# Differential attention of the second layer: scores from two zero-padded copies of the queries, chunk mask added on VectorE

## The reference, cut to what matters

```python
def diff_attention(xn, cos, sin, in_w, q_norm_g, k_norm_g, ..., subln_g, out_w, lambda_init):
    proj = xn @ in_w
    q = proj[..., :1024].reshape(b, s, 8, 2, 64)
    k = proj[..., 1024:2048].reshape(b, s, 8, 2, 64)
    v = proj[..., 2048:].reshape(b, s, 8, 128)
    q = apply_partial_rope(rmsnorm(q, q_norm_g), cos, sin)
    k = apply_partial_rope(rmsnorm(k, k_norm_g), cos, sin)
    scale = 1.0 / math.sqrt(64)
    for blk in range(2):                       # blocks of 128 queries
        qb = q[:, 128 * blk:128 * (blk + 1)]; kc = k[:, :128 * (blk + 1)]
        sc = einsum("bqhcd,bkhd->bhcqk", qb, kc) * scale
        allowed = k_chunk[None, :] <= q_chunk[:, None]      # chunks of 64 tokens
        p = softmax(where(allowed, sc, -inf), axis=-1)
        attn = p[:, :, 0] - lam * p[:, :, 1]
        out_blk = einsum("bhqk,bkhe->bqhe", attn, vc)
    o = rmsnorm(o, subln_g) * (1.0 - lambda_init)
    return o @ out_w
```

## Time and profile before

| | |
|---|---|
| time, median of 3 runs | 1951.2 us (1949.14 to 1953.17) |
| profiled execution | 1950.13 us |
| its span | 1948.4 us |
| PE busy | 1867.1 us (96%) |
| PE weight loads | 1721.3 us (88%) |
| DVE busy | 1351.8 us (69%) |
| ACT busy | 1008.9 us (52%) |
| POOL busy | 5.2 us |
| HBM read | 306.99 MB, 158 GB/s over the span |

### The profile page before, as it was taken

How to read it: one execution, slowest core, us unless ns; L and a number is a source line. 1 busy time by engine, 2 the same in 40 slices (tenths; PEclk the granted TensorE clock), 3 DMA queues, 4 the chain that set the end, 5 groups by cost and what they waited for, 6 DMA issues and landing times.

```text
span 1948.4 us, 32782 instructions
## 1 busy us (share of the span) xinstructions
PE 1867.1 (96%) x12931; PEld 1721.3 (88%) x12931; DVE 1351.8 (69%) x1733; ACT 1008.9 (52%) x1213; POOL 5.2 (0%) x32
## 2 busy tenths in 40 slices
PE   6988999999999899999999999999999999899998
PEld 6988889998878789989999998999989999799997
DVE  6967678888755588877667667666756666657665
ACT  5734455566534465556445435444545445645443
POOL 1000000000000000000000000000000000000000
PEclk8999999999989999999999999999999999999999
DMA  5632145555423245545555554555646554226552
GB/s 186 192 111 107 65 152 187 176 204 174 153 84 108 87 154 191 191 159 189 185 181 173 173 177 149 197 183 180 195 141 205 177 186 157 86 87 203 183 176 85
DMA packets 237638, 309.15 MB, mean 159 GB/s; under 512 B 8186, under 2 KB 213752, under 8 KB 237560
## 3 DMA queue, kind: packets, MB, share of 16 engines
q1 hardware_dynamic: 236520, 308.03, 47.6%
q10 hardware_dynamic: 1040, 0.03, 0.0%
HBM read 306.99 MB, written 1.05 MB: 158 GB/s over the span
## 4 chain that ended last, share of the span: by engine, by line
PE 85%; DVE 8%; ACT 3%; issue 3%; DMA 0%; SPq 0%; DVEq 0%; ACTq 0%
PE ps L599 22%; PE ps L601 11%; PE ps L626 9%; PE ps L628 9%; PE ps L629 9%; PE ps L578 6%; PE ps L580 6%; PE ps L579 6%; DVE weights_lo L1692 2%; ACT weights_hi L1110 1%; PE ps L859 1%; PE ps L806 1%; PE ps L695 1%; DVE scratch L1742 1%; DVE scratch L1738 1%
## 5 line engine op out<-in xcount | busy, mean ns | idle before, releaser
L1692 DVE TENSOR_TENSOR weights_lo<-raw_weights,weights_hi 128x2048 fp32r<-128x2048 f32 x290 | 663.8, 2289 | 252.6 <-ACT weights_hi L1110 252.0
L599 PE MATMUL ps<-normed,weights_hi 128*128 128x512 f32 x2112 | 749.3, 399 | 2.5 <-DVE normed L1775 2.4
L1110 ACT ACTIVATE weights_hi<-raw_weights 128x2048 fp32r<-128x2048 f32 x290 | 551.7, 1905 | 212.1 <-PE ps L580 88.6
L601 PE MATMUL ps<-normed,weights_lo 128*128 128x256 f32 x2112 | 593.3, 281 | 0.0
L599 PEld LDWEIGHTS ps<-normed,weights_hi 128*128 128x128 f32 x2112 | 397.1, 188 | 97.7 <-DVE weights_lo L1692 2.7
L626 PE MATMUL ps<-down_in_hi,weights_hi 128*128 128x256 f32 x1440 | 413.2, 287 | 19.7 <-DVE down_in_lo L1795 7.0
L628 PE MATMUL ps<-down_in_lo,weights_hi 128*128 128x256 f32 x1440 | 412.0, 286 | 0.0
L629 PE MATMUL ps<-down_in_hi,weights_lo 128*128 128x256 f32 x1440 | 411.7, 286 | 0.0
L601 PEld LDWEIGHTS ps<-normed,weights_lo 128*128 128x128 f32 x2112 | 399.7, 189 | 0.1
L578 PE MATMUL ps<-normed,weights_hi 128*128 128x256 f32 x1088 | 322.3, 296 | 10.0 <-DVE normed L1775 7.1
L579 PE MATMUL ps<-normed,weights_hi 128*128 128x256 f32 x1088 | 311.3, 286 | 0.0
(11 more groups left out here) (244 smaller groups left out, 1362.8 us busy)
## 6 DMA issues: line engine op xcount, KB each, us to landing
raw_weights<-in_ffn_w_gate_up_dram SPq DMA_DIRECT2D x88, 1024.0 KB, 5.1
raw_weights<-in_ffn_up_w_dram SPq DMA_DIRECT2D x44, 1024.0 KB, 5.1
raw_weights<-in_ffn_w_down_dram SPq DMA_DIRECT2D x44, 1024.0 KB, 4.9
raw_weights<-in_ffn_down_w_dram SPq DMA_DIRECT2D x22, 1024.0 KB, 4.9
raw_weights<-in_ssd_in_w_dram SPq DMA_DIRECT2D x20, 1024.0 KB, 5.3
raw_weights<-in_a_w_in_dram SPq DMA_DIRECT2D x14, 1024.0 KB, 5.0
raw_weights<-in_attn_in_w_dram SPq DMA_DIRECT2D x12, 1024.0 KB, 5.1
raw_weights<-in_ssd_out_w_dram SPq DMA_DIRECT2D x8, 1024.0 KB, 4.9
```

The lines of the kernel that those rows point to most:

```text
L599: mm(ps[:, b + a, :], wh[:, k, a * P:(a + 1) * P], h[:, k, :, :].rearrange("p c t -> p (c t)"), start=(k == 0), stop=False, skip_group_che ...
L601: last = mm(ps[:, b + a, 0:T], wl[:, k, a * P:(a + 1) * P], h_hi[:, k, :], start=False, stop=(k == DK - 1), skip_group_check=True)
L1110: f(w_hi[:, s, :], raw[:, s, :], ACT.Copy).then_inc(hi_split.sem, hi_split.plus())
L1692: tt(w_lo[:, s, :], raw[:, s, :], f32(w_hi[:, s, :]), ALU.subtract).then_inc(lo_split.sem, lo_split.plus())
```

## The change

The queries exist twice after it, each copy zero in one half of the partitions, so that a product over all 128 partitions gives the score of one of the two queries. ACT makes the copies in `part_queries`, two activations of 128x512 for each pair of heads, during units 5 to 8 of the projection; `halves` holds the two columns of ones and zeros that scale them. PE's four products a step become two over 128 partitions, and the wait on `first_scored` goes. The mask, now a table of 128x256, is added by DVE with the scale of the scores in one operation from PSUM to `s_buf`; the row maxima and the exponentials read `s_buf`. The scale had been part of the query gain. Three more things move: the values of heads 4 to 7 are turned into banks 0 and 1, after the copies of the first ones and without a wait for the rotation; the memory's inverse root is made after unit 11, into `rstd`, ahead of the value copies on ACT; and PE waits for all copies of values, queries and rotated pairs before its first scores. POOL makes two small fills more at the start.

```diff
+            fill(chunk_mask[0:64, P + 64:T], MASKED)
+            fill(halves[0:64, 0:1], 1.0)
+            fill(halves[64:P, 1:2], 1.0)
...
                     if kind == "diff":
-                        mm(ps[:, b, 0:nk], q[0:64, :], proj[0:64, 8 + h, 0:nk], start=True, stop=False,
-                           skip_group_check=True)
-                        late_keys(b, 0, nk, 0).then_inc(first_scored.sem, first_scored.plus())
-                        return
+                        second = second_q[h // 2][:, h % 2, a * P:(a + 1) * P]
+                        mm(ps[:, b, 0:nk], q, proj[:, 8 + h, 0:nk], start=True, stop=True)
+                        last = mm(ps[:, b, T:T + nk], second, proj[:, 8 + h, 0:nk], start=True, stop=True)
...
-            def scores_second(n):
-                if kind == "diff":
-                    h, a, b = n // 2, n % 2, n % 3
-                    nk = keys_of(kind, a)
-                    pe.wait_ge(first_scored.sem, first_scored.value())
-                    mm(ps[:, b, T:T + nk], proj[64:P, q0 + h, a * P:(a + 1) * P], proj[64:P, 8 + h, 0:nk],
-                       start=True, stop=False, skip_group_check=True)
-                    late_keys(b, T, nk, 64).then_inc(scored.sem, scored.plus())
...
             up_unit(first=True)
-            pe.wait_ge(qk_rotated.sem, qk_rotated.next(2))
-            turn_value(1, 2)
+            pe.wait_ge(evacuated.sem, evacuated.value(-1))
+            pe.wait_ge(values_copied.sem, values_copied.next(2))
+            turn_value(1, 0)
...
+            pe.wait_ge(q_parted.sem, q_parted.next(4))
+            pe.wait_ge(qk_rotated.sem, qk_rotated.next(2))
             pe.wait_ge(values_copied.sem, values_copied.next(2))
-            softmax_attention("diff", diff_step, lambda: pe.wait_ge(values_copied.sem, values_copied.next(2)))
+            softmax_attention("diff", diff_step)
...
-                            last = f(p_buf[n % 2][:, j, 0:nk], ps[:, n % 3, j * T:j * T + nk], ACT.Exp,
+                            last = f(p_buf[n % 2][:, j, 0:nk], s_buf[n % 2][:, j, 0:nk], ACT.Exp,
...
+            def part_queries(j):
+
+                act.wait_ge(qk_rotated.sem, qk_rotated.next())
+                q = proj[:, 2 * j:2 * j + 2, :]
+                f(second_q[j], q, ACT.Copy, scale=halves[:, 1:2]).then_inc(step.sem, step.plus())
+                act.wait_ge(step.sem, step.value())
+                f(q, q, ACT.Copy, scale=halves[:, 0:1]).then_inc(q_parted.sem, q_parted.plus())
...
+                if 5 <= n < 9:
+                    part_queries(n - 5)
...
-                if n == 10:
-                    act.wait_ge(stat_done.sem, stat_done.next())
-                    inverse_root(mem_rstd, ps[:, STAT, 0:T], 1.0 / D).then_inc(rstd_ready.sem, rstd_ready.plus())
...
             skip(11, 0)
+            act.wait_ge(stat_done.sem, stat_done.next())
+            inverse_root(rstd[:], ps[:, STAT, 0:T], 1.0 / D).then_inc(rstd_ready.sem, rstd_ready.plus())
             copy_values(TURNED_BEFORE_DIFF, False)
...
                         dve.wait_ge(scored.sem, scored.next())
-                        v.tensor_reduce(t[:, 1, :], bank(n % 3)[:, :, 0:nk], AX_X, ALU.max,
+                        stt(s[:, :, 0:nk], bank(n % 3)[:, :, 0:nk], scale, rows(chunk_mask[:, T - nk:T], 2),
+                            ALU.mult, ALU.add).then_inc(step.sem, step.plus())
+                        dve.wait_ge(step.sem, step.value())
+                        v.tensor_reduce(t[:, 1, :], s[:, :, 0:nk], AX_X, ALU.max,
                                         negate=True).then_inc(shifted.sem, shifted.plus())
```

More of the change, by code:

```diff
@@ L156 @@
 UNITS = sum(s[4] for s in STREAM)
-POOL_MADE = 9 + 2 + ROPE_HALF + 3 + 2 + 4
+POOL_MADE = 10 + 2 + ROPE_HALF + 3 + 3 + 4
 EARLY_EXTRAS, EXTRAS = 4, 9
@@ L219, in build_program @@
         cols = sb("columns", [P, 64])
+        halves = sb("halves", [P, 2])
         eps_col, lam_col, subln_col, freq_col = (cols[:, i:i + 1] for i in range(4))
@@ L276, in build_program @@
         qk_rn = [scr(3840 + 512 * i, 2, T) for i in range(3)]
-        mem_rstd = scr(5376, T)
+        second_q = [scr(5632 + 512 * i, 2, T) for i in range(3)] + [proj[:, 38:40, :]]
         qk_a, qk_b = proj[:, 34:36, :], proj[:, 36:38, :]
-        query_gain = cols[:, 12:13]
         o_rs = [proj[:, 2 * i:2 * i + 2, :] for i in range(4)]
@@ L471, in _ @@
             for m, v in ((ident, 0.0), (ones, 1.0), (upper, 1.0), (half_ones, 0.0), (swap, 0.0),
-                         (chunk_mask, 0.0), (causal_mask, 0.0), (cols, EPS)):
+                         (chunk_mask, 0.0), (causal_mask, 0.0), (halves, 0.0), (cols, EPS)):
                 fill(m[:], v)
@@ L513, in _ @@
             decay_in = c("decay_in")
-            first_scored = c("first_scored")
             evacuated = c("evacuated")
@@ L534, in _ @@
             qk_rotated = c("qk_rotated")
+            q_parted = c("q_parted")
             qk_squares = c("qk_squares")
@@ L799, in ssd_core, with softmax_attention @@
                 square_sum(3, 6, 0)
-            def softmax_attention(kind, between=lambda n: None, ready=lambda: None):
+            def softmax_attention(kind, between=lambda n: None):
                 n_heads, q0, _, _ = attention(kind)
-                def late_keys(b, at, nk, row):
-                    return mm(ps[:, b, at + nk - 64:at + nk], chunk_mask[row:row + 1, 0:P],
-                              chunk_mask[row:row + 1, P:P + 64], start=False, stop=True, skip_group_check=True)
                 def scores(n):
@@ L866, in softmax_attention @@
                     scores(n)
-                    scores_second(n)
-                ready()
                 for n in range(n_units):
@@ L871, in softmax_attention @@
                         scores(n + 2)
-                        scores_second(n + 2)
                     between(n)
@@ L1075, in _ @@
             qk_rstd = c("qk_rstd")
+            qk_rotated = c("qk_rotated")
+            q_parted = c("q_parted")
             qk_squares = c("qk_squares")
@@ L1357, in copy_values @@
                     a, b = (i // 2, i % 2) if by_token else (i % 2, i // 2)
-                    f(v_tok[:, a, 512 * b:512 * b + 512], ps[:, i, :],
+                    f(v_tok[:, a, 512 * b:512 * b + 512], ps[:, i if by_token else a, :],
                       ACT.Copy).then_inc(values_copied.sem, values_copied.plus())
@@ L2208, in finish_tables @@
                 ts(subln_col, vcol("attn_subln_g", 0), 1.0 - LAMBDA_INIT, None, ALU.mult).then_inc(step.sem, step.plus())
-                ts(query_gain, vcol("attn_q_norm_g", 0), ATT_HD ** -0.5, None, ALU.mult).then_inc(step.sem, step.plus())
-                dve.wait_ge(step.sem, step.value())
             def norm_pair(j):
@@ L2215, in norm_pair @@
                 t = proj[:, 2 * j:2 * j + 2, :]
-                stt(t, t, query_gain if j < 4 else vcol("attn_k_norm_g", 0), qk_rn[j % 3],
+                stt(t, t, vcol("attn_q_norm_g" if j < 4 else "attn_k_norm_g", 0), qk_rn[j % 3],
                     ALU.mult, ALU.mult).then_inc(qk_normed.sem, qk_normed.plus())
@@ L2254, in to_memory @@
                    else proj[:, 32 + 4 * l + 2 * i - 4:32 + 4 * l + 2 * i - 2, :], bank(5 - j % 2),
-                   rows(mem_rstd, 2), ALU.mult).then_inc(evacuated.sem, evacuated.plus())
+                   rows(rstd[:], 2), ALU.mult).then_inc(evacuated.sem, evacuated.plus())
             kv_units = woven(KV_WOVEN, to_memory, 1, ahead=True)
```

2 lines of the change are left out of this document (removed).

## The result

| | before | after |
|---|---|---|
| median of the runs | 1951.45 us (4 runs, 1949.14 to 1953.17) | 1921.47 us (4 runs, 1920.66 to 1923.22) |
| ratio after / before | | 0.9847, 95% interval 0.9833 to 0.9861 |
| profiled execution, span | 1950.13 us, 1948.4 us | 1923.22 us, 1921.4 us |
| rotation ends, to step 3's scores | 554.21 to 570.94: 16.7 us | 555.90 to 560.82: 4.9 us |
| step 3's scores to step 13's probability copy | 570.94 to 644.10: 73.2 us | 560.82 to 615.15: 54.3 us |

The kernel is 30.0 us faster at the median, 1.53%. The profiled execution of after is the slowest of its four, so between the two traces 27.0 us are to be found: -11.8, -18.8 and +1.0 us in the three stretches of the table, and +1.7 ahead of them and +1.0 behind, where falls of the granted clock stand in other places.

The account below looks back on a forecast made before the run. PE was taken to bound the kernel, 85% of the chain. Gains of 16.4 us in the scores and 10.9 at the beginning, 27.3 together, took 1950.13 to 1922.8; the median's 1.1 more gave 1924, range 1919 to 1931.

Parts of the forecast that it names:

- The sum: Whole kernel: forecast gain of 27.3 us, from 16.4 us for the scores and 10.9 us at the attention's beginning.
- the two terms of it: PE's score products from step 3 on, 16.4 us gained, and the beginning of the attention, 10.9 us gained.
- The pair of steps: Two attention steps on PE: claimed to shrink from 10.91 to 8.44 us, with PE still setting the pace.
- The two score terms: PE's scores per step: 0.44 us for 128 keys and 0.86 for 256, in place of 1.67 and 2.10.
- the score term: PE's scores of steps 3 to 15: twelve steps give 14.9 us, step 3 gives 1.5, together 16.4 us.
- The fourth rival: PE's score entries: 0.2 us a step stays whatever the products' form, 1927 us; 12% shared with the low-clock rival.
- The beginning: From last rotation to step 3's scores: earlier value turn, 4.9 us at full clock; gain 10.9 us, between 10.1 and 11.7.
- The second rival: Attention's beginning: the low clock holds on, step 3 begins at 562.3, time 1926 us; 12% shared with the entries rival.
- The first rival: Attention's pairs: DVE takes over the pace, 7 pairs lose 0.6 to 1.2 us, about 1930 us; 14%.
- the third: Attention's pairs: the mask on DVE costs more than the products saved, slower, 1955 us or more; 2%.
- The end: Step 13's probability copy to first down product: 9.6 us kept whole; a half-clock stretch may move, 1.6 us either way.
- The edits at no price: Query copies, POOL's fills, weight loads, exponentials from SBUF: claimed to cost nothing; uncovered, the copies would cost 5.4 us.

Follow-up runs that it names:

- e4: Changed kernel with two half-height score products and a wait between them in place of the zero-padded ones, without ACT's query copies; 1930.5 us, ratio to before 0.9890.
- e2: Changed kernel with a one-partition mask product added on PE behind each score product, DVE's mask kept; 1940.9 us, ratio to before 0.9947.
- e9: Kernel before with two needless 128x512 products filling PE's pause ahead of the turn of the second values; 1947.9 us, ratio to before 0.9988.
- e7: Changed kernel with DVE's scale-and-mask operation and its wait done twice in a step; 1924.4 us, ratio to before 0.9873.
- e8: Changed kernel with DVE's scale-and-mask operation and its wait done three times in a step; 1932.0 us, ratio to before 0.9900.
- e1: Changed kernel with the turn of the second values put back behind the last rotation; 1923.0 us, ratio to before 0.9853.
- e11: Changed kernel with PE's sum over heads moved from step 15 to 14 and DVE's norm of heads from step 13 to 15; 1921.4 us, ratio to before 0.9851.
- e3: Kernel before without its mask products, half-height score products and their wait kept; 1937.3 us, ratio to before 0.9927.
- e5: Changed kernel run once more, unaltered, to see whether its beginning repeats; 1922.2 us, ratio to before 0.9854.

## Why the prediction was right, point by point

**The time and the range.** Forecast 1924.0 (1919 to 1931), measured 1921.5. The sum was 27.3 us and the change gave 30.0 at the median, 27.0 between the two traces. That the traces agree with the sum so closely is luck: the two terms of it measured 3.3 us more than forecast, and 3.7 us at the end, ahead and behind, for which the sum had no term, went against them.

**The pair of steps.** The mechanism was right and the size too small: 8.04 us came where 8.44 stood. The two score terms themselves (0.44 and 0.86 us in place of 1.67 and 2.10) hold. What the sum left out is what the old products cost their neighbours. The old price ended where the weights begin, and the first instruction after half height takes 0.22 us until the next starts (566.24 to 566.46 in e4, the line behind those shown), where 0.12 is usual; behind a mask product it is 0.22 too (578.13 to 578.35 in e2), and before ended its scores with one. After has 573.60 - 573.03 = 0.57 us from the scores to the second weight instruction, which is the forecast 0.44 and one such 0.12. On the other side the last two transposes before the scores take 565.28 - 564.97 = 0.31 us in e4 (0.32 in before, 587.40 to 587.72) and 573.03 - 572.81 = 0.22 in after. One tenth at each of the four borders of a pair makes the 0.4 us. Over the stretch the score term was 16.4 us and measured 18.8. "TensorEngine Tiling (Array Packing)" of the Trainium skill, Key Properties, says that a change of the tiling mode drains TensorE; the rows agree, at about 0.1 us each, though they don't show that the drain is the cause. The fourth rival bet on the opposite, that the entries would keep 0.2 us a step in the new form, and it was wrong: they went with the old products.

**The beginning.** The order of events was as forecast: turn behind the weight unit, rotation last, 4.9 us from there to step 3's scores. Forecast gain 10.9, as the middle between a clock that holds (11.7) and one that falls (10.1); measured 11.8, in both traces of the changed kernel. The second rival, a low clock that holds on, did not come: the pause of 1.2 us left the clock at 1.00. The step that failed is the reason given for the old low clock. The prediction laid it to the pause of 1.98 us alone; e9 shows that filling the pause gives back 2.7 of the 11.8 us, and that the clock then falls all the same among the half-height and mask products. That the forecast came out is then partly luck of the sum: it took the new stretch from full-clock rows whatever the cause had been.

**DVE.** 0.42 and 0.69 us forecast, 0.42 and 0.68 measured; its pair of steps 7.2 forecast, 6.70 measured; in the pair from 598.01 to 606.91 us, which has the norm of two heads on DVE and the sum on PE, DVE is busy for 8.62 of 8.90 us. The lead was there: e7 adds another 1.1 us a pair and PE's pair stays 8.04. The first rival needs two more masks to come true (e8), and the third, slower than before, nothing near: e8, with three masks, is still 1% faster than before.

**The end.** The prediction kept it whole and added that a half-clock stretch in it could move, 1.6 us either way. Both held. Step 15's mask and maximum are done before the high split ends (616.20 + 0.69 = 616.9; the split, started at 615.43 behind the copy, takes 1.90 and ends at 617.3). What it did not see is that they stand ahead of step 14's combination in DVE's queue, for which PE asks next and now waits 1.49 us. This wait costs next to nothing, since step 15's chain ends later anyway: e1 has it and takes 9.65 us where before took 9.57. All but 0.1 of the 1.0 us by which after is longer is the moved clock fall: with the clock at 0.50, the sum of squares (L950) takes 1.59 us in after for 1.02 in e1 and before, and the products behind it take longer too. The sum had no term for it, and the range did.

**The edits at no price.** Right in the traces: e1, with the query copies, ends its last rotation at 554.46 us, e4, without them, at 554.66. POOL's two fills put PE's first transposes at 8.31 us for 8.02, and its next work at 16.73 for 16.86.

**What stays open.** How much of the 0.5 us that e4 pays between its two products is the wait and how much the height; and what two half-height products would cost side by side in two banks in every step. How much of the fall among the mask products in e2 and e9 comes from their being thin, and how much from the work and the pauses before, isn't separated either. The clock's falls at the attention's end and elsewhere in the program, which move a run by some microseconds, have no cause here.

## What to carry to other kernels

Small products between large ones cost PE more than their own columns: count the time from the product before to the product after, at each change of height, and put a mask on an engine that idles if it has more slack than the mask is long. Zero-padding an operand to the full height can be cheaper than halving the height, even at the same number of columns, where the two halves would have to wait for each other. When an engine that is off the path gets work, walk its queue at the end of the stage as well, where nothing covers it. A wait that appears there need not cost anything, if another chain ends later; compare with a trace that has the same wait at another clock before you put a price on it.

## What the runs showed of the hardware

PE's granted clock fell to 0.50 (1.2 GHz) while PE was recorded as 94 to 100% busy: in e2 at about 558.5 us (until 565.3) and in e9 at about 558.5 (until 568.7), both times among score products with one-partition mask products between them; the last pause before had been 1.22 us in e2 and 0.26 in e9. Where the masks were gone and the pause ahead of the attention was 1.17 to 1.22 us, it held at 1.00 (after, e4 to e8, e11), half-height products included. After a pause of about 2 us there it fell in every trace, masks or not: before, e1 and e3. At the attention's end a pause is no such sign: behind a wait of 1.49 us the clock fell in after and e5 and held in e1, and it held through 2.22 us in e7.

A product over one partition and 64 columns takes 0.36 us until the next instruction starts (571.59 to 571.95 in e2), as long as three instructions of 256 columns in the weight units (0.12 us each, start to start).
